# Which engines wait, and for what, after the last instruction of a transformer layer on eight cores

## The reference

```python
def swiglu(h, w_ffn_in, w_ffn_out):
    gate, up = jnp.split(h @ w_ffn_in, 2, axis=-1)
    return (jax.nn.silu(gate) * up) @ w_ffn_out

def post_norm(res, out, g, b):
    return layer_norm(DEEPNORM_ALPHA * res + out, g, b)
...
        x_mid = post_norm(x, mod_x[2][:, None, :] * mix, ln1_g[layer], ln1_b[layer])
        h2 = modulate(layer_norm(x_mid), mod_x[3], mod_x[4])
        x_new = post_norm(x_mid, mod_x[5][:, None, :] * swiglu(h2, w_ffn_in[layer], w_ffn_out[layer]),
                          ln2_g[layer], ln2_b[layer])
```

## Time and profile before

| | |
|---|---|
| time, median of 3 runs | 973.14 us (973.07 to 973.97) |
| the profiled execution's own time | 973.24 us |
| its span, from the first to the last instruction, slowest core (core 0) | 971.6 us |
| spans of the 8 cores | 965.4 to 971.6 us |
| granted TensorE clock, mean of a core | 0.979 to 0.989 |

### The profile page before, as it was taken

The page is one execution under the profiler, slowest core; times in us unless marked ns, Lnnn a source line. Parts: engine busy times, 40 slices in busy tenths (PEclk is TensorE's granted clock), DMA queues, the critical chain, the costliest instruction groups (busy, mean ns, idle before and its releaser), DMA issues.

```text
span 971.6 us, 15211 instructions; the slowest of 8 cores (965.4 to 971.6 us)
## 1 busy us (share of the span) xinstructions
PE 890.9 (92%) x5273; PEld 426.7 (44%) x5273; DVE 476.4 (49%) x930; ACT 296.4 (31%) x408; POOL 238.9 (25%) x282
## 2 busy tenths in 40 slices
PE   0568998899899999999999999999999999999993
PEld 0324554444444444444444444444444444444442
DVE  2147675376642366567677422221111115777774
ACT  1215555499932223433433411111111111000000
POOL 5024442266532345545444022000000000000000
PEclk9999999999999999999999999999999999999997
DMA  8998976059730033236944159952220004323231
GB/s 172 173 200 206 179 170 98 2 119 167 150 112 0 1 99 108 66 109 147 190 109 109 44 90 161 160 87 44 44 36 9 1 1 152 122 96 130 87 109 45
DMA packets 57964, 99.68 MB, mean 103 GB/s; under 512 B 20896, under 2 KB 21408, under 8 KB 57888
## 3 DMA queue, kind: packets, MB, share of 16 engines
q0 software_dynamic: 21136, 40.44, 26.8%
q1 hardware_dynamic: 36752, 58.25, 19.6%
HBM read 118.14 MB, written 16.78 MB: 139 GB/s over the span
## 4 chain that ended last, share of the span: by engine, by line
PE 78%; DMA 8%; ACT 5%; DVE 3%; issue 3%; POOL 1%; another core or an unknown queue 0%; SPq 0%; DVEq 0%; ACTq 0%; POOLq 0%
PE bank L1078 31%; PE bank L953 17%; PE bank L1209 15%; DMA arena<-wada 6%; PE bank L984 5%; ACT arena L812 3%; PE bank L488 2%; DMA arena<-xh 2%; PE bank L809 1%; PE bank L558 1%; PE bank L805 1%; PE bank L828 1%; PE bank L528 1%; ACT arena L428 1%; PE bank L540 1%
## 5 line engine op out<-in xcount | busy, mean ns | idle before, releaser
L1078 PE MATMUL bank<-arena 128*128 128x512 bf16 x1408 | 304.9, 379 | 0.0
L1078 PEld LDWEIGHTS bank<-arena 128*128 128x128 bf16 x1408 | 137.8, 98 | 166.1 <-issue 0.4
L953 PE MATMUL bank<-arena 128*128 128x512 bf16 x768 | 167.7, 379 | 0.0
L1089 DVE TENSOR_TENSOR arena<-bank,arena 128x512 bf16<-128x512 f32 x88 | 60.6, 691 | 212.4 <-PE bank L1078 202.3
L1209 PE MATMUL bank<-arena 128*128 128x512 bf16 (+1 forms) x748 | 152.2, 366 | 0.0
L1087 ACT ACTIVATE arena<-bank 128x512 f32<-128x512 f32 x88 | 52.0, 594 | 209.3 <-PE bank L1078 208.6
L953 PEld LDWEIGHTS bank<-arena 128*128 128x128 bf16 x768 | 75.1, 98 | 90.4
L1209 PEld LDWEIGHTS bank<-arena 128*128 128x128 bf16 x748 | 73.2, 98 | 79.1
L969 DVE TENSOR_TENSOR arena<-bank,arena 128x512 f32<-128x512 f32 x64 | 43.3, 690 | 84.0 <-PE bank L953 65.5
L812 ACT ACTIVATE arena<-bank 128x1024 bf16<-128x1024 f32 x80 | 76.3, 1026 | 5.3 <-PE bank L809 5.1
L962 ACT ACTIVATE arena<-bank 128x512 f32<-128x512 f32 x64 | 36.7, 591 | 108.9 <-PE bank L953 108.9
(11 more groups left out here) (108 smaller groups left out, 876.0 us busy)
## 6 DMA issues: line engine op xcount, KB each, us to landing
arena<-xh SPq DMA_DIRECT2D x34, 512.0 KB, 6.0
arena<-wada POOLq DMA_DIRECT2D x12, 1024.0 KB, 16.6
arena<-wff POOLq DMA_DIRECT2D x11, 1024.0 KB, 11.0
xmid_d<-arena SPq DMA_DIRECT2D x16, 512.0 KB, 2.9
arena<-xmid_d SPq DMA_DIRECT2D x16, 512.0 KB, 3.7
out<-arena SPq DMA_DIRECT2D x32, 256.0 KB, 2.2
arena<-wff POOLq DMA_DIRECT2D x11, 512.0 KB, 21.5
arena<-wout SPq DMA_DIRECT2D x16, 256.0 KB, 6.7
```

The source lines that it names most:

```text
L953: t_mm = S.op('pe', lambda e, k=k, n=n, p=bk(bank), lhs=w[:, lo + k, :], rhs=src[:, k, tok]: e.matmul(p, lhsT=lhs, rhs=rhs, start=(k == 0) ...
L1078: rhs=h2T[:, k, tok]: e.matmul(p, lhsT=lhs, rhs=rhs, start=(k == 0), stop=(k == 7)),
L1089: fb_free[b0 + 1] = sg_free[s_] = t_act[(f, tg)] = S.op('dve', lambda e, f=f, p=bk(b0 + 1), sg=sgb[s_]: e.tensor_tensor(out=act[f][:, tok] ...
```

## The change

`barrier` is dropped from `Sched`, and a method `wait` takes its place, which puts one entry of waits on one engine's list. `finish` uses it on SP alone, for the output stores (`final_ticks` holds the stores of all 16 tiles) and for debug stores, of which this program has none. The other four engines' lists now end with their last instruction, and go from there to the closing barrier of `Block`.

```diff
--- before.py
+++ after.py
@@ -70,13 +70,8 @@
         self.q[eng].append((ws, fn, 'dma:' + key, 16))
         return ('dma:' + key, self.dmacnt[key])
 
-    def barrier(self):
-        ticks = [(e, c) for e, c in self.cnt.items() if c > 0]
-        ticks += [('dma:' + k, c) for k, c in self.dmacnt.items()]
-        for e in self.ENG:
-            ws = self._resolve(e, ticks)
-            if ws:
-                self.q[e].append((ws, None, None, 0))
+    def wait(self, eng, deps):
+        self.q[eng].append((self._resolve(eng, deps), None, None, 0))
 
     def emit(self, nc, es):
         sems = {}
@@ -1266,7 +1261,7 @@
         dt_ = spec[2] if len(spec) > 2 else F32
         d = nc.dram_tensor("dbg_" + name, list(shape), dt_, kind="ExternalOutput").ap()
         dbg_ticks.append(S.dma('sp', lambda e, d=d, ap=ap: e.dma_start(out=d, in_=ap), 'dbg', deps=final_ticks))
-    S.barrier()
+    S.wait('sp', [final_ticks, dbg_ticks])
     S.emit(nc, es)
     es.close()
     return nc
```

## The result

The kernel with the change takes 965.94 us as the median of 5 runs, the kernel before 973.14 us in 5 runs beside it. Executions in which a die ran at a lower clock are left out of all ratios here; one of the five, at 980.62 us, is such, and the median of the other four is 965.05 us. The ratio so taken is 0.9912, with a 95% interval of 0.9897 to 0.9928, so 8.6 us less (7.0 to 10.0). Faster was forecast, by 7.9 us, to 965.3.

What follows compares the result with a forecast made beforehand. PE is busy 92% of the span, but its end holds 8.5 us of bookkeeping behind the landing. 963.1 + 0.27 + 0.1 + 0.2 = 963.7 against 971.6 gains 7.9; 973.24 - 7.9 = 965.3 us, range 964.3 to 967.4.

Steps and rivals of the forecast that it cites:

- The bound: End of the span: 8.5 us behind the last output store's landing are bookkeeping, POOL's list and then its closing DRAIN.
- The lists of PE, DVE and ACT: Closing waits of these engines: removal alone worth nothing, as they end at 966.5 to 967.5, behind POOL's 967.7.
- POOL's list, 4.6 us, and its DRAIN, 3.7 us: End of the program on POOL: without its list, 4.6 us of waits and 3.7 us of DRAIN leave the path.
- The DRAIN behind the load in flight: POOL's closing DRAIN, moved to about 722 us behind its last weight load: taken as 3.7 us, hidden under 240 us.
- SP's six waits, its DRAIN and the barrier: Behind the landing at 963.1: waits 0.27 us, to the DRAIN 0.1, gather and release 0.2, so span end 963.7.
- Outside the span: Measured time beyond the profiled span: the 1.64 us there were assumed to stay.
- POOL's DRAIN stays on the path: Rival at the closing barrier: DRAIN is a wait that stays; only 4.3 us go, 968.9 us; chance 0.06.
- The end hangs on the landing: Rival at the span's end: it follows the output's landing by a fixed time; no change, 973.1 us; chance 0.04.
- The stall at the branch: Rival at SP's branch to the closing barrier: fetching the target's code costs about 2.0 us, 967.3 us; chance 0.03.
- Slower: Rival at POOL's last weight load: the early DRAIN holds it back and PE waits; at 60 us, 978 us; chance 0.02.

Runs made afterwards that it cites:

- the run with two waits: The change, but POOL waits for the last tile's two stores before the closing barrier; ratio to the kernel before 0.9947 (0.9931 to 0.9964).

## Why the prediction was right

**The bound.** It said that 8.5 us behind the landing are bookkeeping: POOL's list, then POOL's DRAIN. Both were taken away one at a time. Without the DRAIN's length the tail is 7.1 to 7.5 us; without the lists but with the DRAIN behind the landing it is 6.1 to 6.2 us; without both 2.6 to 2.7. That PE, at whose door the view of waits had put it, had no part in it, is shown by the run in which PE's, ACT's and DVE's lists went and nothing was won.

**The lists of PE, DVE and ACT: worth nothing by themselves.** Right for the end (ratio 0.9996). With POOL out of the way ACT's list was next, as its row said, and stood for 4.2 us of tail (6.9 less 2.7, the slower landing of the stores in it).

**POOL's list, 4.6 us, and its DRAIN, 3.7 us.** Right. 66 ns for a wait was 63 to 64 in two other kernels. The DRAIN, where it still stood behind the landing, was 3667 ns.

**The DRAIN behind the load in flight.** Of three values (173 ns, 3.7 us, 8.9 us) I took 3.7 us as the nearer row. It was 9.8 to 11.0 us: the third was right in kind. The sum didn't hang on it, as said, because 230 us of other work lie over it. With less work behind POOL's last DMA the wrong value would have counted. The argument that 3667 ns on eight cores "looks like a fixed routine" was too strong: the same instruction takes 34 to 201 ns once another DRAIN stands ahead of it. That all cores show the same number fits their having the same program behind them, but what sets it no run shows.

**SP's six waits, its DRAIN and the barrier.** Forecast 963.7 - 960.81 = 2.9 us of tail, measured 2.6 to 2.7. The term that was off is the landing, 2.2 us by the earlier trace rows and 2.0 us now; it went with the lists of the other engines, by a cause that is open. The five satisfied waits were 0.3 us, and reversing the order gave back 0.2 to 0.3. One sum of the prediction doesn't come out: 965.3 with 0.2 and 0.9 us to either side is 964.2 to 966.4, not 964.3 to 966.6. The 965.94 measured lies in both.

**Outside the span** it was 1.64 us before and is 963.71 - 962.2 = 1.5 us; nothing was given back there.

**The rivals.** *POOL's DRAIN stays on the path* would have shown a long DRAIN on POOL at the end; it is at 720. The Trainium skill (page "VectorE: DVE Perf Modes", section "The DRAIN you can't avoid") gives its constant of about 12 ns for the DRAINs that the runtime adds ahead of a program and behind it. The prediction took this as a rule for the DRAINs of the kernel's own `Block`, and for these it doesn't hold: on POOL they took from 34 to 11232 ns, and in the changed kernel PE's took 2155 ns, DVE's 1397 and ACT's 306. DVE's now starts while the last instruction runs and ends with it, 958.1 + 1.4 = 959.5. *The end hangs on the landing* fell with the run with two waits. *The stall at the branch* didn't occur: SP's DRAIN stands at 961.9, where its last wait does. *Slower* would have needed a load held back by 47 us; it landed in 9.1.

## What to carry to other kernels

When the span ends well behind the last computing instruction, list the queue instructions there by engine and time: the last to reach the closing barrier sets it, and that need not be the one that the view of waits names. A wait that is long satisfied still cost 54 ns on SP and 66 on POOL here, so let one engine wait for what the program must not leave behind, and put the newest event last. Where POOL itself has to wait at the end, give it a DRAIN where it is idle, behind its last DMA issue: here the closing one then took 41 ns and not 3667.

## What the runs showed of the hardware

- A satisfied wait is 17 ns in its record and 63 to 66 ns in the time from one to the next on POOL, 54 ns on SP (73 waits in 3.9 us in two kernels).
- POOL's DRAIN took 34 to 46 ns with nothing new on POOL since the last DRAIN, 129 ns behind one small DMA that had landed, 201 to 203 ns behind a memset, and 3667 or 3668 ns as the first one behind the kernel's work on POOL, 65 DMAs among it, though all had landed. As the first one with a 1 MB load in flight it took 9.8 to 11.8 us over all kernels, and ended 1.8 to 1.9 us behind that load's landing. What the 3667 ns are made of is open.
- DVE's closing DRAIN took 1397 ns right behind DVE's last instruction, and ended with it; behind a list of waits it took 17 ns.
- The last stores land in 2.0 us on most cores of the kernels in which PE, ACT and DVE have no closing waits (in the change's second profile three cores of eight had 2.2), and mostly in 2.2 to 2.5 us, with single issues up to 731 ns where 332 is usual, in those in which they have. The cause is open.
